# The up projection of four feed-forward layers in one 512-column product with a ScalarE copy and a VectorE add

## The reference

```python
def swiglu(h, w_gu, w_down):
    g, u = jnp.split(h @ w_gu, 2, axis=-1)
    return (jax.nn.silu(g) * u) @ w_down
...
    for l in range(DEPTH):
        ng = norm_gains[l]
        x = x + FFN_RES_WEIGHT * rms_norm(swiglu(rms_norm(x, ng[0]), ffn_w_gu[l, 0], ffn_w_down[l, 0]), ng[1])
...
        x = x + FFN_RES_WEIGHT * rms_norm(swiglu(rms_norm(x, ng[4]), ffn_w_gu[l, 1], ffn_w_down[l, 1]), ng[5])
```

## Time and profile before

| what | value |
|---|---|
| three runs | 3841.53, 3844.82, 3851.13 us (median 3844.82) |
| the profiled execution, its own time = its span | 3847.5 us |
| TensorE (PE) busy | 3634.0 us, 94% |
| VectorE (DVE) busy | 2690.3 us, 70% |
| ScalarE (ACT) busy | 1712.1 us, 44% |
| the four feed-forward networks | about 14 to 202, 405 to 591, 602 to 787 and 926 to 1116 us |

### The profile page before, as it was taken

One profiled execution on the slowest core, in us unless ns is written; L12 is line 12 of the kernel. 1 busy time (PEld: TensorE's weight loads), 2 busy tenths in 40 slices (PEclk: granted clock), 3 DMA queues, 4 the chain that ended last, 5 costly groups with the idle time before them and its releaser, 6 DMA issues. The chain is left out here.

```text
span 3847.5 us, 59578 instructions
## 1 busy us (share of the span) xinstructions
PE 3634.0 (94%) x22573; PEld 3237.5 (84%) x22573; DVE 2690.3 (70%) x5249; ACT 1712.1 (44%) x2748; POOL 709.4 (18%) x672
## 2 busy tenths in 40 slices
PE   8997999989999986899999999999988899999998
PEld 8895888878878876788899999999976898888887
DVE  5664656656565757897878858888566887777776
ACT  4444445445543544454233323233235554555554
POOL 0001000000010104564344313333010560000000
PEclk9998999999999998899999999999999999999999
DMA  7555656565542123347888858888521466565664
GB/s 266 186 204 226 230 190 220 186 226 198 186 144 103 45 80 121 110 179 280 315 316 303 313 192 310 303 309 317 187 94 50 143 253 229 209 218 208 217 220 164
DMA packets 166774, 793.72 MB, mean 206 GB/s; under 512 B 16896, under 2 KB 58464, under 8 KB 97280
## 3 DMA queue, kind: packets, MB, share of 16 engines
q1 hardware_dynamic: 120496, 603.89, 43.0%
q0 software_dynamic: 45744, 186.36, 13.5%
q10 hardware_dynamic: 288, 0.15, 0.0%
HBM read 740.41 MB, written 47.28 MB: 205 GB/s over the span
## 5 line engine op out<-in xcount | busy, mean ns | idle before, releaser
L247 DVE TENSOR_TENSOR units<-ring,units 128x1024 fp32r<-128x1024 f32 x863 | 1056.4, 1226 | 553.4 <-ACT units L240 544.4
L240 ACT ACTIVATE units<-ring 128x1024 fp32r<-128x1024 f32 x928 | 978.5, 1056 | 991.0 <-PE ps L277 831.1
L276 PE MATMUL ps<-units,weighted 128*128 128x512 f32 x1280 | 501.4, 392 | 0.0
L275 PE MATMUL ps<-units,weighted 128*128 128x512 f32 x1280 | 499.4, 390 | 1.1 <-DVE units L247 1.1
L277 PE MATMUL ps<-units,weighted 128*128 128x512 f32 x1280 | 500.3, 391 | 0.0
L275 PE MATMUL ps<-wide_four,units 128*128 128x384 f32 (+1 forms) x1240 | 406.8, 328 | 6.3 <-PEq L3731 4.9
L277 PE MATMUL ps<-wide_four,units 128*128 128x384 f32 (+1 forms) x1240 | 405.0, 327 | 0.0
L276 PE MATMUL ps<-wide_four,units 128*128 128x384 f32 (+1 forms) x1240 | 404.6, 326 | 0.0
L277 PEld LDWEIGHTS ps<-units,weighted 128*128 128x128 f32 x1280 | 240.2, 188 | 51.2
L275 PEld LDWEIGHTS ps<-units,weighted 128*128 128x128 f32 x1280 | 240.8, 188 | 46.2 <-DVE units L247 1.5
L276 PEld LDWEIGHTS ps<-units,weighted 128*128 128x128 f32 x1280 | 240.7, 188 | 43.5
(11 more groups left out here) (594 smaller groups left out, 8068.4 us busy)
## 6 DMA issues: line engine op xcount, KB each, us to landing
ring<-in_stream SPq DMA_DIRECT2D x469, 1024.0 KB
quad_ring<-in_mod_w POOLq DMA_DIRECT2D x12, 4096.0 KB, 13.9
gates_dram<-gates_place SPq DMA_DIRECT2D x20, 2048.0 KB
gates_place<-gates_dram SPq DMA_DIRECT2D x15, 1536.0 KB
gates_place<-gates_dram SPq DMA_DIRECT2D x15, 1024.0 KB
gain_rows<-in_norm_gains SPq DMA_DIRECT2D x6, 512.0 KB, 4.4
peer_keys<-in_keys SPq DMA_DIRECT2D x3, 1024.0 KB, 6.4
gates_place<-gates_place SPq DMA_DIRECT2D x20, 128.0 KB
```

What stands on the lines that cost most here:

```text
L240: act.activation(K.parts(n)[0], K.raw(n), ACT.Copy).then_inc(K.sig("hi_made").sem, units_to(K, n))
L247: dve.tensor_tensor(lo, K.raw(n), hi.bitcast(FP32), ALU.subtract).then_inc(K.sig("unit_split").sem, units_to(K, n))
L275: pe.matmul(out, w[0], x[0], start=start, stop=False)
L276: pe.matmul(out, w[0], x[1], start=False, stop=False)
```

## The change

The up product takes the gate's form: per k one product of 512 columns and one of 256 in place of three of 256. Its sum then lies in two halves, so ScalarE copies the second half (new tile `up_low`) and VectorE adds it to the first (new tile `up_whole`), and `split_product` reads `up_whole` in place of PSUM. In `step` the order moves: on ScalarE the high part of up f+1 and the new copy stand ahead of `ahead.scalar_step`; on VectorE the low part of up f+1 and the new addition stand ahead of `split_product`, so also ahead of `ahead.vector_step`.

```diff
@@ feed_forward
         act_out = K.sbuf("silu", [P, 2, SEQ], ctx=local)
         gate = K.sbuf("gate_whole", [P, 2, SEQ], ctx=local)
+        low = K.sbuf("up_low", [P, 2, SEQ], ctx=local)
+        risen = K.sbuf("up_whole", [P, 2, SEQ], ctx=local)
         gated, halved = K.sig("gated"), K.sig("pair_raised")
+        up_halved, up_summed = K.sig("pair_weighed"), K.sig("pair_shared")
@@ up
-                    if m == 0:
-                        both = K.ps[:, 4 + 2 * (f % 2), :]
-                        pe.matmul(both, weight[0][:, k, :], columns[:, :, k, :], start=(k == 0), stop=False)
-                        last = pe.matmul(both[:, 0:SEQ], weight[1][:, k, :], columns[:, 0, k, :], start=False, stop=(k == KD - 1))
-                        continue
-                    last = product3(pe, K.ps[:, 4 + 2 * (f % 2) + m, 0:SEQ], [w[:, k, :] for w in weight],
-                                    [columns[:, h, k, :] for h in range(2)], k == 0, k == KD - 1)
+                    both = K.ps[:, 4 + 2 * (f % 2) + m, :]
+                    pe.matmul(both, weight[0][:, k, :], columns[:, :, k, :], start=(k == 0), stop=False)
+                    last = pe.matmul(both[:, 0:SEQ], weight[1][:, k, :], columns[:, 0, k, :], start=False, stop=(k == KD - 1))
@@ scalar step
                     act.activation(act_out[:, f % 2, :], gate[:, f % 2, :], ACT.Silu).then_inc(silued.sem, 1)
+                    if f < FT - 1:
+                        split_hi(K, act, n0 + up_unit(f + 1) + 1, i)
+                    act.wait_ge(unit_used, n0 + up_unit(f) + 2 + i * BODY_UNITS)
+                    act.activation(low[:, f % 2, :], K.ps[:, 5 + 2 * (f % 2), SEQ:2 * SEQ], ACT.Copy).then_inc(up_halved.sem, 1)
                     if ahead is not None and isinstance(i, int):
                         ahead.scalar_step(act, f)
-                    if f < FT - 1:
-                        split_hi(K, act, n0 + up_unit(f + 1) + 1, i)
                     split_hi(K, act, n0 + down_unit(f), i)
@@ vector step
-                    dve.wait_ge(unit_used, n0 + up_unit(f) + 2 + i * BODY_UNITS)
+                    if f < FT - 1:
+                        split_lo(K, dve, n0 + up_unit(f + 1) + 1, i)
+                    dve.wait_ge(up_halved.sem, up_halved.base + f + 1 + i * TILES_BODY)
+                    dve.tensor_tensor(risen[:, f % 2, :], low[:, f % 2, :], K.ps[:, 5 + 2 * (f % 2), 0:SEQ], ALU.add)\
+                       .then_inc(up_summed.sem, 1)
                     dve.wait_ge(silued.sem, silued.base + f + 1 + i * TILES_BODY)
-                    split_product(dve, whole[:, f % 2, :], hid[:, f % 2, :, :], act_out[:, f % 2, :],
-                                  K.ps[:, 5 + 2 * (f % 2), 0:SEQ], hidden, f, i * TILES_BODY)
+                    dve.wait_ge(up_summed.sem, up_summed.base + f + 1 + i * TILES_BODY)
+                    split_product(dve, whole[:, f % 2, :], hid[:, f % 2, :, :], act_out[:, f % 2, :], risen[:, f % 2, :],
+                                  hidden, f, i * TILES_BODY)
                     if ahead is not None and isinstance(i, int):
                         ahead.vector_step(dve, f)
-                    if f < FT - 1:
-                        split_lo(K, dve, n0 + up_unit(f + 1) + 1, i)
                     split_lo(K, dve, n0 + down_unit(f), i)
```

More of the change, by code:

```diff
@@ L1736, in feed_forward @@
     K.taken += FFN_SLOTS
+    up_halved.past(FT), up_summed.past(FT)
     silued.past(FT), gated.past(FT), halved.past(FT), hidden.past(STEPS * FT), K.sig("pair_scored").past(1)
```

## The result

The change takes 3864.95 us, the median of four runs (3862.41 to 3866.39), beside 3844.78 us for four runs of the kernel before: a ratio of 1.005, 95% interval 1.0036 to 1.0064. It is slower by some 20 us where 11.9 were forecast, and 1 us above the range.

What follows compares the result with a forecast made beforehand. TensorE's stream of columns was taken to bound the networks. The walk's +7.6 us and the clock's +4.3 gave +11.9 on the profiled 3847.5, so 3859.4, or 3856.7 us for a median; range 3848 to 3864.

Steps and rivals of the forecast that it cites:

- the term for the products: Up products in 88 tiles of four networks take the gate's time, 0.04 us less each: 3.5 us less (1.8 to 4.4).
- tiles 18 to 20: Fourth network: helper's columns come behind low part and addition, TensorE 2.1 us late in three tiles: 6.3 us more.
- head of the fourth network: Scales before gate 2 come later, TensorE idle 3.1 us; up 1's wait goes: 1.9 us more (1.2 to 2.6).
- four ends: Last tile of each network: last down unit's split comes behind the new work: together 2.9 us more (2 to 4).
- clock: Four new TensorE idle gaps bring 2.6 falls to granted clock 0.50, 1.65 us each: 4.3 us more (0 to 6.6).
- this rival: Clock stays up at the four gaps, time not measurably slower; two or fewer falls, at most 10.9 us more; chance 0.18.
- The steady tiles: Loop tiles keep 3 to 4 us of slack and cost nothing; rival of lost cover: 3897 us, chance 0.04.
- a saving of 0.15 us a tile: Rival that the new form saves more in the products: 13 us, sum near -1; chance 0.02.

Runs made afterwards that it cites:

- the form alone: Kernel before with only the up unit's two products in the new form, no copy or addition, old order, part of the sum left out: 3845.97 us, one run.
- the tiles alone: Kernel before with the change's two new tiles reserved but unused, so later tiles lie where the change puts them: 3844.20 us, one run.
- The order alone: Kernel before with only the change's order on ScalarE and VectorE, no new form, copy or addition: 3849.6 us, one run.
- its gaps filled: The change with transposes into an unused bank in TensorE's idle time before gates 2 and 19 to 21 of the fourth network: 3858.54 us.
- the head's gap filled: The change with 24 transposes into an unused bank where TensorE waits before gate 2 of the fourth network: 3858.16 us, one run.
- the old order: The change with the kernel before's order: helper ahead of up f+1's high and low parts, behind copy, addition and hidden product: 3856.8 us, ratio 1.0036.
- the helper first: The change with helper work right behind the SiLU (tile 0: behind the copy) on ScalarE, behind the gate's addition on VectorE: 3849.82 us, ratio 1.0012.

## Why the prediction was off

The direction, given a chance of 0.52, and the places were right; **the step that failed is the term for the products, -3.5 us**. It gives the up product the gate's shorter time and leaves the gate's own time as it was. The runs show that the saving stays away in networks 2 to 4, where the gate slows down instead: the term is -0.6 us in the first profiles and about +0.3 with the form alone. By the steps, from the two first profiles:

| term | forecast | measured |
|---|---|---|
| products | -3.5 | -0.6 |
| tiles 18 to 20 | +6.3 | +6.6 |
| head of the fourth network | +1.9 | +2.1 |
| four ends | +2.9 | +3.6 |
| clock | +4.3 | +3.2 |
| sum | +11.9 | +14.9 |

- **Products.** The reading was right: before, the gate takes 0.03 to 0.04 us less than the up product in all four networks. But the price didn't carry over. In the first network the up product goes from 2.85 to 2.81 us, as forecast; in networks 2 to 4 it stays at 2.82 (2.79 to 2.81 forecast), and the gate, whose products the change doesn't touch, goes from 2.80 to 2.82. The gate's length was no property of its form alone. The measured -0.6 is what is left of the 14.9 after the other terms: about -2 in the first network, of which 1.0 is its first tile, which varies from execution to execution, and +0.4 to +0.5 in each of the others; in the other two profiles of the change the remainder is +0.1 and +0.7. The form alone beside the tiles alone, without that first tile, gives -0.9 and +0.4 in each of the others. By the Trainium skill (TensorE: Matmul & The Clock Gate, section "Wait — 56ns, not 53.3ns?"), with a fixed time on each matmul, 8 fewer had to save something; networks 2 to 4 show no such saving, at 5.64 us for 32 matmuls and 5.62 for 40.
- **Tiles 18 to 20.** From one gate to the next, 11.00, 11.11 and 11.09 us in place of 8.86, 8.88 and 8.86; the idle time of 1.96 us lies in the forecast 1.8 to 2.2, and the releaser is the forecast one. The order alone makes 1.4 us of each idle time; the rest comes with the new work.
- **The head.** Gate 2 begins 17.7 us after the network's start in place of 15.6. The idle time forecast at 3.1 us is 3.08.
- **The ends.** Idle times of 0.58 us in networks 2 and 3 (0.65 forecast) and of 1.41 and 1.42 in 1 and 4 (over 1 forecast); with the products around them, 0.85 to 0.95 us each.
- **The clock.** Two falls in every profile of the change where 2.6 were forecast, at 1.6 us each (202.8 against 199.6 with none) where 1.65 was. The clock did not stay up, and the network with its gaps filled shows that the idle gaps were the cause. But the prediction lets this rival decide at the third fall, and two falls lie on the rival's side: that the runs are clearly slower all the same comes from the products' term and from the 5.3 us below. The Trainium skill (same page, section "HAM oscillation — how this bites in real kernels") has only longer gaps bring the clock down; the measurement, 0.50 behind gaps of 1.96 to 1.98 us, is against it.
- **The steady tiles** cost nothing beyond the 0.02 us: no wait appears in them.
- **A slip in the rivals.** With a saving of 0.15 us a tile the walk comes to -2.1 us, not near -1.

The terms make 3.0 of the 8.3 us between forecast and result (11.9 above the kernel before, and 20.2). With nothing for the products the forecast would have been +15.4, near the 14.9 of the networks. The other 5.3 come from which executions were compared: the one profiled before stood 4.5 us above its median (3849.3 against 3844.8), the one of the change 0.8 below. The rest of the program took 3099.2 us in both. Over all profiles it goes from 3092.4 to 3101.2 us, whatever the kernel.

**What stays open.** Over all runs beside the change and the experiments, 54 of the kernel before and 14 of the change, the means are 3843.7 and 3862.8 us: 19.1 us apart, with a standard error near 1. By batches, the medians are 20.2, 20.6 and 14.3 us apart. The networks of three profiles of the change give 14.9 to 16.2. Whether the remaining 3 to 4 us are more falls in the timed runs than the two that profiles show, something in the rest of the program, or in part chance, these runs don't settle. The mean granted clock of the timed runs is lower for the change (0.9774 against 0.9794). At two levels that is an estimated 16 us more at 0.50 in an execution, of which two falls of 3.4 us are 7; the other 9 would cost some 4 us if TensorE were dense there. But where they lie isn't shown, and the two first profiles warn against it: the change's has 7 us more at 0.50 outside the networks, and the rest of the program took as long in both.

## What to carry to other kernels

- An instruction's shorter time beside another's is not yet a price: it can hang on the stream around it. Here the saving of one product was lost on its neighbour in three networks of four. Build the one form alone, and look at both products, before a saving is counted 88 times.
- Work that has cover in the steady loop may have none at the places where a helper's results are waited for. Walk those tiles on each in-order engine; the same change cost 14.9 us of network time as it stood and 4.6 with the helper's calls ahead of the moved work.
- A profiled execution has its own place in the spread of the runs. Sum against its stage times, and take the runs' median for the whole.

## What the hardware showed that was not expected

- **Columns, not the number of matmuls, set the pace to within 1% in networks 2 to 4**: the 1536 columns of each k in 4, 5 or 6 matmuls took 5.64, 5.62 and 5.65 us a tile. Only in the first network did fewer, wider products help at each step, 5.62, 5.65 and 5.70.
- **The same products have more than one pace at the same granted clock**: the wide up product took 2.79 us in tile 2 of the third network and 2.82 from tile 3 on, and in networks 2 to 4 the gate took 2.80 beside a narrow up product and, in most tiles, 2.82 beside a wide one. The granted clock was 1.00 in all of these.
- **Short idle gaps between dense stretches bring the clock down, but not each time**: of the three of 1.94 to 1.99 us one was followed by 0.50 in each profile of the change and two with the head's gap filled; the gap of 3.08 to 3.12 us was each time. Gaps of 1.4 us in the order-alone run were not, its gap of 2.28 us was, and so were the 1.96 us of the old order and the 1.99 us of the helper first. Filled with transposes, none was in the one profile of it, though the same products began as late.
